# First norm of each layer and the input projection: two stages before, one stage after

## The chip, the cores and the metric

The kernel runs on one core of a Trainium2 chip. A core has five engines that run side by side and wait for one another by semaphores: TensorE (matmuls; PE in the profile, its weight loads PEld), VectorE (DVE), ScalarE (ACT), GpSimd (POOL) and SyncE (SP), which here only issues transfers (its queue is SPq). 16 DMA engines move the data. Matmuls accumulate in eight banks of PSUM, and VectorE or ScalarE copy each result out ("evacuation"). The metric is the time on the device in microseconds, the median of several runs. The profile is of one execution.

## The reference, cut to what matters

Two layers work on 1280 tokens of 1024 features: 256 context tokens and 1024 image tokens. Each layer begins with a norm and a projection:

```python
h = modulate(rmsnorm(x, norm_mix_g[l]), sh1, sc1)          # image tokens
hc = modulate(rmsnorm(xc, norm_mix_g[l]), csh1, csc1)      # context tokens, other shift and scale
parts = split_cols((h @ w_in).astype(F32))                 # 2608 columns
parts_c = split_cols((hc @ (w_in if ctx_out else w_in[:, :REC_W])).astype(F32))
...
qk = jax.nn.silu(conv2d_grid(jnp.concatenate([parts[5], parts[6]], axis=-1), conv_w, rows, cols))
```

`rmsnorm` divides by the root of the mean of the squares over a token's 1024 features; `modulate` multiplies by 1 + scale and adds shift. `ctx_out` is true in layer 0 only: in layer 1 the context tokens need no columns for the chunked gating and the Fourier mixing. Everything is float32. Mixers, output projection, a dense feed-forward part (layer 0), a mixture of eight experts (layer 1) and a final norm follow.

## The kernel before

`build` (L1976) calls one function per stage. A stage is a `Phase` (L113): a block in which each engine has its own program, and at its end a barrier of all engines; GpSimd then clears the stage's semaphores one by one. No transfer of a stage is issued before the stage ahead of it has ended. Data lies feature-major: 128 partitions, `KD` = 8 chunks of features, tokens along the row. The tokens come in three groups, `GROUPS` (L32): 256 context tokens, 512 image tokens, 512 image tokens.

`phase_norm` (L256) is the first of the two stages. SyncE loads the three groups of x (1, 2 and 2 MB) into `xT`, which lies in the space of `TM` (L271). For each group ScalarE squares eight chunks into a ring of four (L282), TensorE multiplies each square with a matrix of ones, which sums it over the partitions (L303), VectorE makes the mean plus epsilon (L312), ScalarE the root (L289), VectorE the reciprocal (L314) and the scaled chunks in place (L317), and ScalarE adds the shift and writes `hT` (L293). ScalarE's order is written out: the squares of a group stand ahead of the root and the shifts of the group before it.

`phase_project` (L322) is the second. A unit, called a tile here, is one PSUM bank: eight matmuls that sum over the chunks. Units "fm" (L400) give 128 output columns for one group of tokens, feature-major, into `FM`; units "tm" (L403) give 128 tokens by 512 columns, token-major, into `TM`. The weights come in seven blocks (four fm: q and k of the first mixer, the conv's input, the Fourier mixer's input, the gates; three tm) into a ring of two slots; a block's load waits until the last unit of the block two before it is done (L367). The gates' slot is zeroed by GpSimd first (L386), and its columns come in five small transfers (L373). The conv's taps come in four (L380). All 57 units (53 in layer 1) go block by block, context and image in each block. They use eight PSUM banks in turn; ScalarE evacuates the even units and VectorE the odd ones (L412). Between its evacuations VectorE does the 3x3 conv in twelve parts (`taps_of`, L429: four chunks, three rows of taps), and ScalarE the Silu behind it (L421).

Of the kernel before, what the change touches and what calls it, by code (L numbers as in the profile page):

```python
# [18 lines left out]
ACT = mybir.ActivationFunctionType  # L19
ALU = mybir.AluOpType  # L20
# [298 lines left out]
                            in1=rstd[:, g % 2, :n], op0=ALU.mult, op1=ALU.mult).then_inc(scaled, 1)  # L319


def phase_project(nc, io, S, l, hT, FM, TM, ctx_out):  # L322


    loads = [((0, 256), [0, 1]), ((800, 512), [2, 3, 4, 5]), ((2352, 256), [6, 7]), (None, [8])]
    tok = [(256, 0), (1312, 512), (1840, 1024)]
    w_in = io["w_in"][l].rearrange("(k p) n -> p k n", p=P)
    units = []
    for i, (_, chunks) in enumerate(loads):
        for j, ch in enumerate(chunks):  # L330
            for t0, n in GROUPS:
                if ch in (6, 7) and not ctx_out and t0 < CTX:
                    continue
                units.append((i, "fm", j, ch, t0, n))
    for i, (_, dst) in enumerate(tok):
        for n in range(NT):
            if dst == 1024 and not ctx_out and n < NCT:
                continue
            units.append((len(loads) + i, "tm", 0, dst, n, 0))
    last_of = {}  # L340
    for u, un in enumerate(units):
        last_of[un[0]] = u
    NB = 8
    with Phase(nc, f"proj{l}") as ph:
        wring = ph.sb("w", [P, 2, KD, 512])
        wl = [ph.sem(f"w_loaded{s}") for s in range(2)]
        taps = ph.sb("taps", [P, 4, 9])
        y = ph.sb("y", [P, 2, T])
        mm_done, ev = ph.sem("mm_done"), [ph.sem("evacuated_act"), ph.sem("evacuated_dve")]
        zeroed, tl, ch, cv, silu_done = (ph.sem(n) for n in ("gate_slot_zeroed", "taps_loaded", "dve_step", "convolved", "silu_done"))  # L350
        ps = S["ps"]
        nl = len(loads) + len(tok)
        cnt = {}
        need = []
        for i in range(nl):
            s = i % 2
            cnt[s] = cnt.setdefault(s, 0) + (5 if i == 3 else 1)
            need.append(16 * cnt[s])

        with nc.Block() as block:  # L360

            @block.sync
            def _(sp):
                for i in range(nl):
# [3 lines left out]
                    if i == 3:  # L368

                        sp.wait_ge(zeroed, 1)  # L370
                        with nc.allow_non_contiguous_dma(reason="gate columns"):
                            for dst, src, n in ((0, 1824, 4), (4, 1832, 4), (32, 1828, 4), (36, 1836, 4), (64, 768, 32)):
                                sp.dma_start(wring[:, s, :, dst:dst + n], w_in[:, :, src:src + n]).then_inc(wl[s], 16)  # L373
                    else:
                        c0, n = loads[i][0] if i < len(loads) else (tok[i - len(loads)][0], 512)
                        sp.dma_start(wring[:, s, :, 0:n], w_in[:, :, c0:c0 + n]).then_inc(wl[s], 16)
                    if i == 1:
                        with nc.allow_non_contiguous_dma(reason="taps as columns"):
                            for j in range(4):
                                sp.dma_start(taps[:, j, :], io["mlstm_conv"][l].rearrange("a b d -> (a b) d")[:, j * P:(j + 1) * P]  # L380
                                             .rearrange("t p -> p t")).then_inc(tl, 16)

            @block.gpsimd
            def _(pool):
                pool.wait_ge(mm_done, last_of[1] + 1)
                nc.gpsimd.memset(wring[:, 1, :, 0:P], 0.0).then_inc(zeroed, 1)  # L386

            @block.tensor
            def _(pe):
                seen = -1  # L390
                for u, (i, kind, j, dst, a, n) in enumerate(units):
                    if i != seen:
# [14 lines left out]
            def evacuate(eng, copy, u):  # L407
                i, kind, j, dst, a, n = units[u]
                eng.wait_ge(mm_done, u + 1)
                out = FM[:, dst, a:a + n] if kind == "fm" else TM[:, a, dst:dst + 512]  # L410
                src = ps[:, u % NB, :n] if kind == "fm" else ps[:, u % NB, :]
                copy(out, src).then_inc(ev[u % 2], 1)  # L412

            @block.scalar
            def _(act):
                for u in range(0, len(units), 2):
                    evacuate(act, nc.scalar.copy, u)
                    j = u // 6 - 3
                    if u % 6 == 0 and 0 <= j < 4:
                        act.wait_ge(cv, j + 1)  # L420
                        nc.scalar.activation(FM[:, 2 + j, :], y[:, j % 2, :], ACT.Silu).then_inc(silu_done, 1)  # L421
                act.wait_ge(ev[0], (len(units) + 1) // 2)
                act.wait_ge(silu_done, 4)

            @block.vector
            def _(dve):
                step = Chain(dve, ch)

                def taps_of(j, dr):  # L429
                    x, o = FM[:, 2 + j, :], y[:, j % 2, :]  # L430
                    x2, o2 = (a[:, CTX:].rearrange("p (r c) -> p r c", c=GRID_W) for a in (x, o))
                    if dr == 0:
                        dve.wait_ge(ev[0], (9 + 3 * j + 1) // 2)
                        dve.wait_ge(ev[1], (9 + 3 * j) // 2)
# [20 lines left out]
                for u in range(1, len(units), 2):  # L455
                    evacuate(dve, nc.vector.tensor_copy, u)
                    part = (u - 11) // 2
                    if 0 <= part < 12:
                        taps_of(part // 3, (0, -1, 1)[part % 3])
                for j in range(2):  # L460
                    dve.wait_ge(silu_done, j + 1)

                    step(nc.vector.tensor_scalar(FM[:, 2 + j, :], FM[:, 2 + j, :], HD ** -0.5, None, ALU.mult))
                dve.wait_ge(ev[1], len(units) // 2)


# [1620 lines left out]
```

## Time and profile before

| | us |
|---|---|
| median of 3 runs | 6105.13 (6094.68 to 6106.96) |
| profiled execution | 6100.45 |
| its span in the trace | 6098.5 |
| TensorE busy in the span | 5281.8 (87%) |
| VectorE busy | 2772.0 (45%) |
| ScalarE busy | 2003.3 (33%) |
| mean granted TensorE clock | 0.924 of full speed |

The time of the profiled execution is 2 us over its span. "Busy" counts the time in which an engine executes an instruction; matmuls are pipelined, so a busy TensorE is not one at its peak. A granted clock of 1.00 is 2.4 GHz and one of 0.50 is 1.2 GHz; a value between them means that a stretch had both. The two stages of layer 0 lie from 137 to 559 us of the span, those of layer 1 from 2206 to 2607.

### The profile page before, as it was taken

The numbers are of one execution on the slowest core, as the hardware profiler recorded it, in microseconds if no ns is written. First come the engines' busy times: TensorE is split into PE (matmuls) and PEld (weight loads), VectorE is DVE, ScalarE is ACT, GpSimd is POOL, SyncE is SP. The second block draws the span as 40 slices with busy tenths as digits, with TensorE's granted clock in tenths as the row PEclk, the third lists the DMA queues.
The fourth block names the chain that finished last, engine by engine and source line by source line (L and its number), as shares of the span: only waits on it lengthen the run. The fifth ranks groups of instructions, "written<-read, shape, count | busy, mean of one in ns | idle before, by whom it ended". The sixth has DMA issues, their size and how long they took to land. (4 is left out here: it accounts for less than half of the span.)

```text
span 6098.5 us, 61033 instructions
## 1 busy us (share of the span) xinstructions
PE 5281.8 (87%) x22972; PEld 3997.5 (66%) x22973; DVE 2772.0 (45%) x2881; ACT 2003.3 (33%) x1980; POOL 163.6 (3%) x239
## 2 busy tenths in 40 slices
PE   6899395699997969967576999999999999999994
PEld 2444174588886744425465888877887888887883
DVE  0220474311113332126524644699558644448566
ACT  1100111211112220011112534577447534437453
POOL 0000020000000000001101000000000000000001
PEclk8899697799998989978786999999999999999996
DMA  9111003211215431010227755699669755558575
GB/s 377 29 43 54 15 1 136 84 56 60 63 35 183 136 131 36 14 64 1 90 104 297 297 186 199 242 365 367 228 224 355 275 186 200 199 186 333 200 264 220
DMA packets 262623, 996.66 MB, mean 163 GB/s; under 512 B 40000, under 2 KB 112384, under 8 KB 175744
## 3 DMA queue, kind: packets, MB, share of 16 engines
q1 hardware_dynamic: 243200, 926.43, 41.4%
q0 software_dynamic: 13040, 49.29, 2.2%
q10 hardware_dynamic: 6288, 19.66, 0.8%
q8 instruction: 61, 1.00, 0.1%
q14 instruction: 34, 0.28, 0.0%
HBM read 911.68 MB, written 83.63 MB: 163 GB/s over the span
## 5 line engine op out<-in xcount | busy, mean ns | idle before, releaser
L1696 PE MATMUL ps<-moe_gate_up_hi,moe_xh 128*128 128x512 f32 x2464 | 964.9, 392 | 29.1 <-DVE moe_gate_up_lo L1841 29.1
L1696 PE MATMUL ps<-moe_gate_up_hi,moe_xl 128*128 128x512 f32 x2464 | 962.9, 391 | 0.0
L1696 PE MATMUL ps<-moe_gate_up_lo,moe_xh 128*128 128x512 f32 x2464 | 962.6, 391 | 0.0
L1841 DVE TENSOR_TENSOR moe_gate_up_lo<-moe_wst,moe_gate_up_hi 128x2048 fp32r<-128x2048 f32 x424 | 952.8, 2286 | 20.1 <-ACT moe_gate_up_hi L1774 20.1
L1774 ACT CAST moe_gate_up_hi<-moe_wst 128x2048 fp32r<-128x2048 f32 x424 | 792.1, 1922 | 0.0
L1854 DVE TENSOR_TENSOR moe_down_lo<-moe_wst,moe_down_hi 128x2048 fp32r<-128x2048 f32 x210 | 480.6, 2292 | 165.3 <-ACT moe_down_hi L1788 165.3
L1696 PEld LDWEIGHTS ps<-moe_gate_up_hi,moe_xh 128*128 128x128 f32 x2464 | 465.4, 189 | 128.3 <-DVE moe_gate_up_lo L1841 31.4
L1696 PEld LDWEIGHTS ps<-moe_gate_up_hi,moe_xl 128*128 128x128 f32 x2464 | 464.9, 189 | 97.3
L1696 PEld LDWEIGHTS ps<-moe_gate_up_lo,moe_xh 128*128 128x128 f32 x2464 | 465.3, 189 | 96.5
L1860 DVE TENSOR_TENSOR moe_a<-moe_sil,ps 128x512 f32<-128x512 f32 x210 | 143.9, 685 | 753.6 <-ACT moe_sil L1794 753.6
L1794 ACT ACTIVATE moe_sil<-ps 128x512 f32<-128x512 f32 x210 | 126.0, 600 | 1032.2 <-PE ps L1696 1032.0
L1716 PE MATMUL ps<-moe_down_hi,moe_ah 128*128 128x512 f32 x1232 | 403.1, 408 | 30.6 <-DVE moe_al L1865 30.6
L1256 PE MATMUL ps<-hh,up_wh 128*128 128x512 f32 (+1 forms) x1056 | 376.8, 357 | 51.2 <-DVE up_wl L1300 39.4
L1788 ACT CAST moe_down_hi<-moe_wst 128x2048 fp32r<-128x2048 f32 x210 | 403.7, 1922 | 22.8 <-PE ps L1716 22.7
L403 PE MATMUL ps<-proj_w,hT 128*128 128x512 f32 x928 | 398.6, 592 | 0.0
L1716 PE MATMUL ps<-moe_down_lo,moe_ah 128*128 128x512 f32 x1232 | 386.1, 395 | 0.0
L1716 PE MATMUL ps<-moe_down_hi,moe_al 128*128 128x512 f32 x1232 | 383.6, 393 | 0.0
L1256 PE MATMUL ps<-hl,up_wh 128*128 128x512 f32 (+1 forms) x1056 | 374.4, 355 | 0.0
L1256 PE MATMUL ps<-hh,up_wl 128*128 128x512 f32 (+1 forms) x1056 | 374.2, 354 | 0.0
L400 PE MATMUL ps<-hT,proj_w 128*128 128x512 f32 (+1 forms) x832 | 307.6, 533 | 48.5 <-DMA proj_w<-in_w_in 48.5
L403 PEld LDWEIGHTS ps<-proj_w,hT 128*128 128x128 f32 x928 | 176.3, 190 | 221.9 <-issue 221.9
L400 PEld LDWEIGHTS ps<-hT,proj_w 128*128 128x128 f32 x832 | 161.3, 194 | 194.9 <-issue 136.8
(329 smaller groups left out, 6497.9 us busy)
## 6 DMA issues: line engine op xcount, KB each, us to landing
moe_wst<-in_moe_packed SPq DMA_DIRECT2D x634, 1024.0 KB, 6.7
ada_w<-in_ada_packed SPq DMA_DIRECT2D x24, 2048.0 KB, 26.5
down_wst<-in_ffn_w_down SPq DMA_DIRECT2D x66, 512.0 KB, 3.6
proj_w<-in_w_in SPq DMA_DIRECT2D x8, 2048.0 KB, 7.9
four_dft<-in_dft_seq SPq DMA_DIRECT2D x16, 1024.0 KB, 4.9
xs_d<-route_zero SPq DMA_DIRECT2D x1, 16384.0 KB, 51.8
moe_rows<-xs_d POOLq DMA_DIRECT2D x16, 1024.0 KB, 5.6
ys_d<-moe_y POOLq DMA_DIRECT2D x15, 1024.0 KB, 8.5
```

The lines of the kernel that those rows point to most:

```text
L400: mm = nc.tensor.matmul(ps[:, u % NB, :n], wring[:, i % 2, k, j * P:(j + 1) * P], hT[:, k, a:a + n], start=(k == 0), stop=(k == KD - 1))
L403: mm = nc.tensor.matmul(ps[:, u % NB, :], hT[:, k, a * P:(a + 1) * P], wring[:, i % 2, k, :], start=(k == 0), stop=(k == KD - 1))
L1256: x = nc.tensor.matmul(ps[:, 2 * g + kind, :n], w[:, s, kind, k, :], h[:, k, t0:t0 + n], start=(k == 0 and j == 0), stop=(k == KD - 1 and ...
L1696: x = nc.tensor.matmul(ps[:, 2 * (q % 2) + i, :], xx[:, k, t], w[:, q % 2, k, :], start=(k == 0 and j == 0), stop=(k == KD - 1 and j == 2))
L1716: x = nc.tensor.matmul(ps[:, Y0 + 2 * i + half, :], aa[:, q % 2, i, c, :], w[:, q % 2, c, half * 512:(half + 1) * 512], start=(q == 0 and ...
L1774: nc.scalar.copy(guh[:, q % 2, 4 * j:4 * j + 4, :], wst[:, slot(n), :].rearrange("p (k n) -> p k n", k=4)).then_inc(hi, 1)
L1788: nc.scalar.copy(dnh[:, q % 2, :, :], wst[:, slot(n), :].rearrange("p (k n) -> p k n", k=2)).then_inc(hi, 1)
L1794: nc.scalar.activation(sil[:, :, :], ps[:, 2 * (q % 2):2 * (q % 2) + 2, 0:W], ACT.Silu).then_inc(silu, 1)
L1841: nc.vector.tensor_tensor(gul[:, q % 2, k, :], wst[:, slot(n), :].rearrange("p (k n) -> p k n", k=4), guh[:, q % 2, k, :].bitcast(F32), AL ...
L1854: nc.vector.tensor_tensor(dnl[:, q % 2, :, :], wst[:, slot(n), :].rearrange("p (k n) -> p k n", k=2), dnh[:, q % 2, :, :].bitcast(F32), AL ...
L1860: nc.vector.tensor_tensor(a[:, q % 2, :, :, :].rearrange("p i c f -> p i (c f)"), sil[:, :, :], ps[:, 2 * (q % 2):2 * (q % 2) + 2, W:2 * W ...
```

## The change

The two stages become one, `phase_norm_project`. x is loaded straight into `hT` and scaled and shifted there in place. The squares' ring lies in the space of `y` (the conv's buffer). One PSUM bank, number 7, is kept for the variances, and the units go round in the other seven. SyncE issues the first blocks of weights between the groups of x. The units are put in a new order: first all context units, block by block (15 in layer 0; 11 in layer 1, which has no context units in two of the blocks), then the image units of the conv's and the gates' blocks, which are in the slots at that point, then the other five blocks loaded again with their image units. The matmuls of the third group's variance stand ahead of the third unit. ScalarE alternates between a square of the next group and a shift of the present one. The number of matmuls, squares, shifts and evacuations stays.

```diff
-def phase_project(nc, io, S, l, hT, FM, TM, ctx_out):
-    loads = [((0, 256), [0, 1]), ((800, 512), [2, 3, 4, 5]), ((2352, 256), [6, 7]), (None, [8])]
-    tok = [(256, 0), (1312, 512), (1840, 1024)]
...
-    NB = 8
+def phase_norm_project(nc, io, S, l, src, hT, FM, TM, ctx_out):
+    NB, VAR = 7, 7
...
+    fm = {"qk": (0, 256, [0, 1]), "conv": (800, 512, [2, 3, 4, 5]), "four": (2352, 256, [6, 7]), "gates": (None, P, [8])}
+    tm = {"t0": (256, 512, 0), "t1": (1312, 512, 512), "t2": (1840, 512, 1024)}
+    only_out = ("four", "t2")
+    first = [n for n in ("qk", "t0", "t1", "t2", "four", "conv", "gates") if ctx_out or n not in only_out]
+    second = ["qk", "t0", "t1", "t2", "four"]
+    loads = first + second
+    GATES = len(first) - 1
+    uses = [(i, n, GROUPS[:1]) for i, n in enumerate(first)]
+    uses += [(GATES - 1, "conv", GROUPS[1:]), (GATES, "gates", GROUPS[1:])]
+    uses += [(len(first) + i, n, GROUPS[1:]) for i, n in enumerate(second)]
...
+                load_x(0)
+                for i, name in enumerate(loads):
                     s = i % 2
                     if i >= 2:
                         sp.wait_ge(mm_done, last_of[i - 2] + 1)
...
+                    if i == 0:
+                        load_x(1)
                     if i == 1:
+                        load_x(2)
...
             @block.tensor
             def _(pe):
+                def variance(g):
+                    n = GROUPS[g][1]
+                    if g:
+                        pe.wait_ge(var_ready, g)
+                    for k in range(KD):
+                        q = g * KD + k
+                        pe.wait_ge(sq_ready, q + 1)
+                        nc.tensor.matmul(ps[:, VAR, :n], ones, sq[:, q % 4, :n], start=(k == 0), stop=(k == KD - 1)).then_inc(sq_used, 1)
+
+                variance(0)
+                variance(1)
                 seen = -1
                 for u, (i, kind, j, dst, a, n) in enumerate(units):
+                    if u == 0:
+                        pe.wait_ge(shifted, KD)
+                    if u == 2:
+                        variance(2)
+                    if u == image:
+                        pe.wait_ge(shifted, 3 * KD)
...
             @block.scalar
             def _(act):
...
+                for k in range(KD):
+                    square(0, k)
+                for g in range(2):
+                    deviation(g)
+                    for k in range(KD):
+                        square(g + 1, k)
+                        shift(g, k)
+                evacuate(act, nc.scalar.copy, 0)
+                evacuate(act, nc.scalar.copy, 2)
+                deviation(2)
+                for k in range(KD):
+                    shift(2, k)
+                for u in range(4, len(units) + 8, 2):
...
             @block.vector
...
+                scale(0)
+                scale(1)
+                evacuate(dve, nc.vector.tensor_copy, 1)
+                scale(2)
...
-                    xT = TM[:, 0:7, :].rearrange("p a b -> p (a b)")[:, 0:KD * T].rearrange("p (k t) -> p k t", t=T)
-                    phase_norm(nc, S, f"nm{l}", io["xT"] if l == 0 else S["xT_d"], xT, hT, l, 0, GROUPS)
-                    phase_project(nc, io, S, l, hT, FM, TM, ctx_out)
+                    phase_norm_project(nc, io, S, l, io["xT"] if l == 0 else S["xT_d"], hT, FM, TM, ctx_out)
```

The order of instructions shows it on three engines, each at the start of the norm in layer 0. TensorE before (L303 are the variance's matmuls, L400 the first units; `cst` is the matrix of ones, `nm_sq` the squares):

```order
L303 MATMUL ps<-nm_sq,cst 128x256 [waits nm0_sq_ready] x8
L303 MATMUL ps<-nm_sq,cst 128x512 [waits nm0_sq_ready] x16
L266 UNCONDITIONAL_BRANCH
L388 UNCONDITIONAL_BRANCH [waits barrier_Pool_Activation_PE_DVE_SP_release]
L400 MATMUL ps<-hT,proj_w 128x256 [waits proj0_w_loaded0]
L400 MATMUL ps<-hT,proj_w 128x256 x7
```

And now (L423 the variance, L443 the fm units, L446 the tm units; the squares lie in `proj_y`):

```order
L423 MATMUL ps<-proj_y,cst 128x256 [waits proj0_sq_ready] x8
L423 MATMUL ps<-proj_y,cst 128x512 [waits proj0_sq_ready,proj0_var_ready]
L423 MATMUL ps<-proj_y,cst 128x512 [waits proj0_sq_ready] x7
L443 MATMUL ps<-hT,proj_w 128x256 [waits proj0_w_loaded0,proj0_shifted]
L443 MATMUL ps<-hT,proj_w 128x256 x15
L423 MATMUL ps<-proj_y,cst 128x512 [waits proj0_sq_ready,proj0_var_ready]
L423 MATMUL ps<-proj_y,cst 128x512 [waits proj0_sq_ready] x7
L446 MATMUL ps<-proj_w,hT 128x512 [waits proj0_w_loaded1]
```

The barrier between variance and units is gone, and the third group's eight variance matmuls have moved behind the first two units, ahead of the third.

ScalarE before (L282 squares, L289 root, L293 shifts):

```order
L282 ACTIVATE nm_sq<-TM 128x512 [waits nm0_sq_used] x7
L289 ACT_TABLE_LOAD
L289 ACTIVATE nm_rstd<-nm_rstd 128x256 [waits nm0_var_ready]
L293 ACTIVATE hT<-TM,mod 128x256 [waits nm0_scaled] x8
L282 ACTIVATE nm_sq<-TM 128x512 [waits nm0_sq_used,nm0_x_loaded2]
```

And now (L467 squares, L472 root, L477 shifts):

```order
L467 ACTIVATE proj_y<-hT 128x256 [waits proj0_sq_used] x4
L472 ACT_TABLE_LOAD
L472 ACTIVATE proj_rstd<-proj_rstd 128x256 [waits proj0_var_ready]
L467 ACTIVATE proj_y<-hT 128x512 [waits proj0_sq_used,proj0_x_loaded1]
L477 ACTIVATE hT<-hT,mod 128x256 [waits proj0_scaled]
L467 ACTIVATE proj_y<-hT 128x512 [waits proj0_sq_used]
L477 ACTIVATE hT<-hT,mod 128x256 [waits proj0_scaled]
```

The context root and the context shifts have moved ahead of, and in between, the second group's squares.

SyncE's queue in the joint stage of layer 0, up to the second pass (L384 x, L398 and L395 weights, L405 taps); before, the three x loads were a stage of their own:

```order
L384 DMA hT<-in_xT 128x8x256
L398 DMA proj_w<-in_w_in 128x8x256
L384 DMA hT<-in_xT 128x8x512
L398 DMA proj_w<-in_w_in 128x8x512
L384 DMA hT<-in_xT 128x8x512
L405 DMA proj_taps<-in_mlstm_conv 128x9x1 x4
L398 DMA proj_w<-in_w_in 128x8x512 [waits proj0_mm_done] x2
L398 DMA proj_w<-in_w_in 128x8x256 [waits proj0_mm_done]
L398 DMA proj_w<-in_w_in 128x8x512 [waits proj0_mm_done]
```

Two blocks of weights have moved in between the x loads.

## Rows read from the trace of the kernel before

**Rows 1.** The page's costliest groups: feature-major projection matmuls, busy, mean ns, idle before.

```profile
L400 PE MATMUL ps<-hT,proj_w 128*128 128x512 f32 (+1 forms) x832 | 307.6, 533 | 48.5 <-DMA proj_w<-in_w_in 48.5
```

**Rows 2.** Table by stretches: length, busy time and count of each engine, granted clock, DMA.

```profile
162.20:166.30 4.10, 4.01 (x5) 1.78 (x6) 0.00 (x0) 2.42 (x6) 0.00 (x0) 0.53 0.00 0
166.30:170.70 4.40, 4.40 (x12) 1.90 (x10) 1.66 (x1) 2.21 (x4) 0.00 (x0) 1.00 0.00 0
170.70:195.40 24.70, 0.56 (x3) 0.01 (x1) 16.42 (x19) 11.24 (x17) 0.00 (x0) 0.61 0.18 56
195.39:199.60 4.21, 4.21 (x10) 3.41 (x11) 0.00 (x0) 0.00 (x0) 0.00 (x0) 0.50 1.05 388
...
352.50:558.70 206.20, 206.17 (x481) 91.01 (x479) 26.83 (x31) 11.13 (x17) 0.00 (x0) 1.00 0.06 21
```

**Rows 3.** SyncE's queue in layer 0: start, duration, issues.

```profile
137.14 3.68 SPq L271 DMA_DIRECT2D TM<-in_xT  x3
190.03 1.02 SPq L376 DMA_DIRECT2D proj_w<-in_w_in  x2
...
302.21 3.59 SPq L373 DMA_DIRECT2D proj_w<-in_w_in  x5
```

**Rows 4.** TensorE in layer 0, 130 to 215 us, in order of time.

```profile
162.29 8.97 PE L303 MATMUL ps<-nm_sq,cst 128*128 128x512 f32 x16 [5.17 <-ACT nm_sq L282]
195.39 19.79 PE L400 MATMUL ps<-hT,proj_w 128*128 128x256 f32 x48 [24.14 <-DMA proj_w<-in_w_in]
```

**Rows 5.** ScalarE in layer 0's norm, in order of time.

```profile
143.73 1.33 ACT L282 ACTIVATE nm_sq<-TM 128x256 f32<-128x256 f32 x4 [12.20 <-DMA TM<-in_xT]
...
149.16 3.47 ACT L282 ACTIVATE nm_sq<-TM 128x512 f32<-128x512 f32 x6 [0.73 <-DMA TM<-in_xT]
...
154.36 1.28 ACT L289 ACT_TABLE_LOAD   x1
155.66 0.42 ACT L289 ACTIVATE nm_rstd<-nm_rstd 128x256 f32<-128x256 f32 x1
158.41 3.30 ACT L293 ACTIVATE hT<-TM,mod 128x256 f32<-128x256 f32 x8 [2.34 <-DVE TM L317]
...
173.21 5.36 ACT L293 ACTIVATE hT<-TM,mod 128x512 f32<-128x512 f32 x8 [4.21 <-DVE TM L317]
...
183.30 5.36 ACT L293 ACTIVATE hT<-TM,mod 128x512 f32<-128x512 f32 x8 [4.21 <-DVE TM L317]
```

**Rows 6.** VectorE in layer 0's norm, in order of time.

```profile
150.28 0.42 DVE L312 TENSOR_SCALAR nm_rstd<-ps 128x256 f32<-128x256 f32 x1 [14.94 <-PE ps L303]
...
157.89 3.26 DVE L317 SCALAR_TENSOR_TENSOR TM<-TM,gmod,nm_rstd 128x256 f32<-128x256 f32 x8
...
169.04 3.35 DVE L314 RECIPROCAL nm_rstd<-nm_rstd 128x512 f32<-128x512 f32 x1 [7.28 <-ACT nm_rstd L289]
```

**Rows 7.** Transfers, issue to landing: x (137), first weights (190), token-major weights (335).

```profile
TM<-in_xT SPq DMA_DIRECT2D x1, 1024.0 KB, 6.6
...
proj_w<-in_w_in SPq DMA_DIRECT2D x1, 2048.0 KB, 10.7
proj_w<-in_w_in SPq DMA_DIRECT2D x1, 1024.0 KB, 5.3
...
proj_w<-in_w_in SPq DMA_DIRECT2D x1, 2048.0 KB, 7.8
```

**Rows 8.** A conv part on VectorE (first and last row) and GpSimd's memset.

```profile
301.76 1.05 DVE L437 TENSOR_SCALAR proj_y<-FM,proj_taps 128x1280 f32<-128x1280 f32 x1
...
305.97 0.49 DVE L449 SCALAR_TENSOR_TENSOR proj_y<-FM,proj_taps,proj_y 128x255 f32<-128x255 f32 x1
...
L386 POOL MEMSET proj_w<- x2: 956/956/956, 301.2 to 2369.7; 128x1024 f32 x2
```

**Rows 9.** Layer 1: first x load, first projection matmul.

```profile
2205.86 2.98 SPq L271 DMA_DIRECT2D TM<-xT_d  x3
...
2263.96 26.63 PE L400 MATMUL ps<-hT,proj_w 128*128 128x256 f32 x72 [24.36 <-DMA proj_w<-in_w_in]
```

More of the change, by code:

```diff
@@ L319, in _ @@
                             in1=rstd[:, g % 2, :n], op0=ALU.mult, op1=ALU.mult).then_inc(scaled, 1)
-def phase_project(nc, io, S, l, hT, FM, TM, ctx_out):
-    loads = [((0, 256), [0, 1]), ((800, 512), [2, 3, 4, 5]), ((2352, 256), [6, 7]), (None, [8])]
-    tok = [(256, 0), (1312, 512), (1840, 1024)]
+def phase_norm_project(nc, io, S, l, src, hT, FM, TM, ctx_out):
+    NB, VAR = 7, 7
     w_in = io["w_in"][l].rearrange("(k p) n -> p k n", p=P)
-    units = []
[L329 to L342, printed above, removed]
-    NB = 8
+    fm = {"qk": (0, 256, [0, 1]), "conv": (800, 512, [2, 3, 4, 5]), "four": (2352, 256, [6, 7]), "gates": (None, P, [8])}
[8 more added lines that the diff above has]
+    uses += [(len(first) + i, n, GROUPS[1:]) for i, n in enumerate(second)]
+    units = []
+    for i, name, groups in uses:
+        if name in fm:
+            for j, ch in enumerate(fm[name][2]):
+                for t0, n in groups:
+                    units.append((i, "fm", j, ch, t0, n))
+        else:
+            for t0, n in groups:
+                for tile in range(t0 // P, (t0 + n) // P):
+                    units.append((i, "tm", 0, tm[name][2], tile, 0))
+    last_of = {un[0]: u for u, un in enumerate(units)}
+    image = min(u for u, un in enumerate(units) if un[1] == "fm" and un[4] >= CTX)
+    conv_in = [max(u for u, un in enumerate(units) if un[1] == "fm" and un[3] == 2 + j) for j in range(4)]
+    part_at, at = [], 0
+    for j in range(4):
+        for r in range(3):
+            at = max(at, conv_in[j])
+            at += 1 if at % 2 == 0 else 2
+            part_at.append(at)
+    silu_at = [part_at[3 * j + 2] + 3 for j in range(4)]
+    scale_at = [silu_at[j] + 2 for j in range(2)]
@@ L410, in evacuate, with square @@
                 out = FM[:, dst, a:a + n] if kind == "fm" else TM[:, a, dst:dst + 512]
-                src = ps[:, u % NB, :n] if kind == "fm" else ps[:, u % NB, :]
-                copy(out, src).then_inc(ev[u % 2], 1)
+                acc = ps[:, u % NB, :n] if kind == "fm" else ps[:, u % NB, :]
+                copy(out, acc).then_inc(ev[u % 2], 1)
             @block.scalar
             def _(act):
[L416 to L421, printed above, removed]
+                def square(g, k):
+                    t0, n = GROUPS[g]
+                    q = g * KD + k
+                    if k == 0:
+                        act.wait_ge(xl[g], 16)
+                    if q >= 4:
+                        act.wait_ge(sq_used, q - 3)
+                    nc.scalar.activation(sq[:, q % 4, :n], hT[:, k, t0:t0 + n], ACT.Square).then_inc(sq_ready, 1)
@@ new lines, in _ @@
+                for k in range(KD):
[11 more added lines that the diff above has]
+                for u in range(4, len(units) + 8, 2):
+                    if u < len(units):
+                        evacuate(act, nc.scalar.copy, u)
+                    for j in range(4):
+                        if silu_at[j] in (u, u + 1):
+                            act.wait_ge(cv, j + 1)
+                            nc.scalar.activation(FM[:, 2 + j, :], y[:, j % 2, :], ACT.Silu).then_inc(silu_done, 1)
@@ L427, in _, with scale @@
                 step = Chain(dve, ch)
+                def scale(g):
+                    t0, n = GROUPS[g]
+                    dve.wait_ge(sq_used, (g + 1) * KD)
+                    if g >= 2:
+                        dve.wait_ge(scaled, KD * (g - 1))
+                    nc.vector.tensor_scalar(rstd[:, g % 2, :n], ps[:, VAR, :n], 1.0 / D, EPS, ALU.mult, ALU.add).then_inc(var_ready, 1)
+                    dve.wait_ge(sd_ready, g + 1)
+                    nc.vector.reciprocal(rstd[:, g % 2, :n], rstd[:, g % 2, :n]).then_inc(rst, 1)
+                    dve.wait_ge(rst, g + 1)
+                    for k in range(KD):
+                        nc.vector.scalar_tensor_tensor(
+                            out=hT[:, k, t0:t0 + n], in0=hT[:, k, t0:t0 + n], scalar=gmod[:, l, 0, (1 if g == 0 else 0), k:k + 1],
+                            in1=rstd[:, g % 2, :n], op0=ALU.mult, op1=ALU.mult).then_inc(scaled, 1)
                 def taps_of(j, dr):
```

68 lines of the change are left out of this document (42 added, 26 removed).

## The prediction, written before the result was known

> **What bounds the kernel now.** The program is a row of stages with a barrier of all engines between them, so I read each stage by itself; the page's shares of busy time average over stages with different limits. Among the page's costliest groups the projection's feature-major matmuls (L400) have 48.5 us of idle TensorE before them, charged to the weight load [rows 1]. That idle time is the norm stage in front of the projection, where TensorE has only 24 small matmuls. The table by stretches shows both sides: from 170.70 to 195.40 us TensorE is busy 0.56 us of 24.7, from 352.5 to 558.7 it is busy all the time at full clock [rows 2]. So the stage pair is bound first by the norm's chain (load, squares on ScalarE, variance on TensorE, root, reciprocal and scale on VectorE, shift on ScalarE) and then by TensorE. In layer 0 the first x load is issued at 137.14 us and the first projection matmul starts at 195.39: 58.25 us [rows 3, 4]. In layer 1 it is 2205.86 to 2263.96, 58.1 us [rows 9].
>
> The unit of the sum: the token-major matmuls, two records each, fill the stretch from 352.5 to 558.7 with 480 records in 206.2 us (481 with one cut at its edge) [rows 2], so a matmul takes 0.859 us and an output tile of eight 6.87 us. A context tile of a feature-major chunk streams half as many columns and takes 3.43 us. Layer 0 has 57 such tiles, of which 15 are context: 6 token-major and 9 feature-major, 6 x 6.87 + 9 x 3.43 = 72.1 us. Layer 1 has 11: 4 x 6.87 + 7 x 3.43 = 51.5 us. The total of TensorE work is not changed.
>
> **The change, step by step, in times of layer 0 before.** *x, first group.* The context x is still the first transfer; the first square stays at 143.73, the variance is read by VectorE at 150.28 and done at 150.70 [rows 5, 6]. What could move it is the 1 MB of weights now queued behind it: nothing if transfers of one queue follow each other, 2.7 us if they share it fully (2 MB take 10.7 less 5.3 = 5.4 us, so 1 MB takes 2.7 [rows 7]). I take 0.
>
> *Root.* Before, the context root waited on ScalarE behind the eight squares of the next group, until 155.66. Now it is ahead of them. The table load (1.28 us) started the moment a square ended, ahead of the waiting instruction [rows 5], so it now runs at 148.4 to 149.7 under the last variance matmuls. The Trainium skill ("ScalarE: Activation LUTs", What ACT_TABLE_LOAD costs) gives a drain of about 1.4 us beside the load of 1.28; the trace agrees on the 1.28 and shows no such gap between load and root, and by the page the sum would still be the same here, since both end before 151.1. The root starts at 150.7; first scale 2.23 us and first shift 2.75 us behind its start, as before (155.66, 157.89, 158.41 [rows 5, 6]), that is 152.9 and 153.5.
>
> *Second group's squares, interleaved with context shifts.* Its x is 2 MB and had landed at 149.16 behind 1 MB; with 1 MB of weights ahead it lands at 151.9, about when ScalarE is free (151.1). Squares follow each other at 3.47/6 = 0.58 us, context shifts at 3.30/8 = 0.41 [rows 5], so a pair takes 0.99 and the eighth square ends at 153.5 + 0.41 + 6 x 0.99 + 0.58 = 160.4. TensorE must follow: after an idle time of some 5 us the clock was 0.53 in a stretch of 4.1 us, then 1.00 [rows 2, 4]. Cold, a variance matmul takes 1.72 us. From 154.5 on it has work without a gap: 4.1 us cold (2.4 matmuls), the other 4.6 at 0.86 give 162.6. Bounds: 161.3 if warm throughout, 166.5 if cold throughout (154.5 + 7 x 1.72). The first projection tile starts at 162.6, its weights long there, and two context tiles end at 169.5.
>
> *Third group's squares, in front of the third tile.* This is the wait that the change adds: TensorE's queue is in order and holds the other 55 tiles behind it. VectorE 0.7, ScalarE's root 0.6, then 4.2 us from the start of the 512-column reciprocal (169.04) to the first shift (173.21) [rows 5, 6]: first image shift at 168.2. The third x lands at 137.14 + 12.0 + 5 MB x 2.7 = 162.7, needed at 164. A pair is 0.58 + 5.36/8 = 1.25 us; the last square ends at 168.2 + 0.67 + 6 x 1.25 + 0.58 = 177.0, the variance at 177.9. Bounds: the same, or 183.3 if TensorE ran cold (169.5 + 8 x 1.72). I take 178.0, since it is busy 0.86 of every 1.25 us.
>
> *What this is worth.* The third tile starts at 178.0. Before, two context tiles' worth of work were done at 195.39 + 6.87 + 2.1 = 204.4, the 2.1 being half of the 4.21 us at clock 0.50 [rows 2]. So 26.4 us are gained. What remains of the norm (third group: evacuation of tile 2 at 185, root, reciprocal, scale, shift: 0.6 + 0.6 + 4.2 + 5.4 = 11 us, ready at 197) lies beside context tiles that last until 178.0 + 65.2 = 243; image tiles need it only then. In layer 1 they last until 178.0 + 44.6 = 222.6 on the same scale, still 25 us spare.
>
> *Weights.* The second pass streams 8 MB again in layer 0 and 5 MB in layer 1 (where the Fourier block and the last token-major block have no context tiles). Each load waits for the last use of its slot and has the other slot's tiles as cover: 13.7 us for the two token-major blocks of layer 0's context, against 7.8 us from issue to landing [rows 7]. One cover is thin: the conv block (2 MB) has only the Fourier block's two context tiles, 6.87 us; 7.8 + 0.3 - 6.9 = 1.2 us of wait, layer 0 only (layer 1 has a token-major block there). Without any cover it would be 8. The gate columns: memset 0.96, five issues in 3.59 us, landing at most the 5.3 of a 1 MB block [rows 3, 7, 8], 9.9 us against 13.7 of cover: 0. In the second pass the thinnest cover is the 13.7 us of the gates' image tiles. The taps stand behind all x loads and are wanted at 197: 0.
>
> *VectorE and the conv.* Its longest part, 301.76 to 306.46, is 4.7 us [rows 8] between evacuations 13.7 us apart; seven accumulators instead of eight leave six tiles of slack. The conv's last activation stands at tile 42 of 57. Cost 0; if a part were late by all seven banks it would have to last 40 us.
>
> *Boundary.* One barrier per layer goes (inside the 26.4), but its ten semaphore clears move to the end of the joint stage. ScalarE's last shift ended at 188.66 and the weights were issued at 190.03, so ten clears and a barrier are 1.37 us at most; I take 0.5 a layer, bounds 0 and 1.4. In-place shifts instead of TM to hT: the scale was in place already (TM from TM) and is no odd row among its neighbours; I take 0.
>
> Sum: layer 0 26.4 - 1.2 - 0.5 (a last bit of cold clock) - 0.5 = 24.2; layer 1 26.4 - 0.2 (58.1 against 58.25) - 0.5 - 0.5 = 25.2; together 49.4. The profiled execution took 6100.45 us, so 6051. The median of the runs is 6105.13, 4.7 above it; the new median may lie anywhere between 6051 and 6056, and I say 6053.
>
> **Rivals.** *A, the chain is slower than back-to-back rows say.* ScalarE now alternates between two producers and each instruction waits on another semaphore; x comes in between weights in one queue. If the second x lands only with the 2 MB of weights behind it (5.4 us), and TensorE stays cold through both variance passes (3.9 and up to 5.4 us), a layer loses 12 to 15 of its 25 us: about 6080; half of it 6066. For it: the clock did fall in the short pause at 157 to 162. Against: the first x landed in 6.6 us with 4 MB behind it.
>
> *B, slower: the clock stays at half in the context pass.* TensorE gets its work there in blocks between waits for squares and weights. The Trainium skill ("TensorE: Matmul & The Clock Gate", HAM oscillation) says that short bursts between waits for transfers start cold each time; our trace shows the same fall once per norm, and no case of bursts of 13 us. If all context tiles ran at 1.2 GHz, 72.1 + 51.5 = 123.6 us would double: 6051 + 124 = 6175. It turns slower than before once 50 of these 124 us are cold. Against it: from the third tile on the waits are nil but for 1.2 us, and in the rows a 4 us stretch of work brought the clock back to 1.00.
>
> *C, no difference.* The norm would have to be on the path again, for instance if the image shifts reached 243; that needs 46 us more on a chain of 11. Or weight loads in the context pass take twice as long (15.5 us against covers of 13.7 and 6.9): 2 + 2 + 9 us in layer 0, 4 in layer 1, and the gain is still about 34: no zero either.
>
> **How the numbers follow.** Forecast (gain 40 to 57) 0.78; A 0.15; B 0.03; C 0.04. A gain of under 12 us, 0.2%, is about what a measurement of this kernel can't tell from no change. Faster 0.93 (forecast and A), within 0.2% 0.04, slower 0.03. The range: upward to A's middle and a bit, 6074; downward all lower bounds (warm 1.3, free x 0.8, no conv wait 1.2, no clears 0.5) give about 6044, and the runs scatter by 12 us between them, so 6039.
>
> **What would show it.** First projection matmul some 25 us behind the first x issue instead of 58; the third tile's at 41 us, with idle TensorE before it put down to ScalarE's squares; idle before the conv context tiles of 1 us put down to the weight load in layer 0, none in layer 1; no idle TensorE after that; granted clock 1.00 from the third tile on. Wrong would be: a wait for image shifts at the first image tile, clock near 0.5 in the context tiles, or idle time in front of the gates' tile.

## The result and the profile after

| | before | after |
|---|---|---|
| median, us (4 runs each) | 6101.79 | 6048.30 (6039.77 to 6049.45) |
| ratio to before, 95% interval | | 0.991 [0.9893, 0.9927] |
| profiled execution: span, us | 6098.5 | 6037.6 |
| mean granted TensorE clock | 0.924 | 0.927 |

The kernel became 53.5 us faster by the medians. The forecast was 6053, range 6039 to 6074. The two profiled executions are 60.9 us apart. The lengths of the two stages, read in the traces from the first x issue to the next stage's first transfer, give 26.6 + 27.9 = 54.5 us of that. The other 6.4 us lie in the rest of the program, which is not changed; in the eleven profiled executions of this document that rest took 5265 to 5284 us. So the length of the stages is the measure below. The kernel after profiled twice (e5) gives it to 0.4 us in each layer, while the span differed by 18 us; e8, with the same instructions in layer 1, was 2.1 us longer there, so differences under 2 us are not read as effects.

SyncE's queue after, layer 0, then layer 1 (start, duration, issues; to be read beside [rows 3, 9]):

```profile
134.40 0.64 SPq L384 DMA_DIRECT2D hT<-in_xT  x1
...
165.73 49.47 SPq L398 DMA_DIRECT2D proj_w<-in_w_in  x4
...
531.30 0.34 SPq L580 DMA_DIRECT2D four_dftc<-in_dft_ctx  x1
...
2175.59 0.55 SPq L384 DMA_DIRECT2D hT<-xT_d  x1
...
2550.42 16.04 SPq L584 DMA_DIRECT2D four_dft<-in_dft_seq  x4
```

Layer 0 takes 531.30 - 134.40 = 396.9 us. Before it was 560.67 - 137.14 = 423.5. Layer 1: 2550.42 - 2175.59 = 374.8 against 2608.55 - 2205.86 = 402.7. The first Fourier transfers before, layer 0, then layer 1:

```profile
560.67 0.34 SPq L484 DMA_DIRECT2D four_dftc<-in_dft_ctx  x1
...
2608.55 1.29 SPq L488 DMA_DIRECT2D four_dft<-in_dft_seq  x3
```

TensorE after, layer 0, in order of time; it answers to [rows 4]:

```profile
141.49 6.10 PE L423 MATMUL ps<-proj_y,cst 128*128 128x256 f32 x16 [9.83 <-ACT proj_y L467]
150.21 8.57 PE L423 MATMUL ps<-proj_y,cst 128*128 128x512 f32 x16 [2.63 <-ACT proj_y L467]
158.62 7.07 PE L443 MATMUL ps<-hT,proj_w 128*128 128x256 f32 x32
165.53 8.07 PE L423 MATMUL ps<-proj_y,cst 128*128 128x512 f32 x16
173.44 41.36 PE L446 MATMUL ps<-proj_w,hT 128*128 128x512 f32 x96
214.64 7.07 PE L443 MATMUL ps<-hT,proj_w 128*128 128x256 f32 x32
222.65 39.85 PE L443 MATMUL ps<-hT,proj_w 128*128 128x256 f32 x132 [0.95 <-DMA proj_w<-in_w_in]
```

The first tile (158.62) starts 24.2 us behind the first x issue (58.25 before), the third (173.44) 39.0. In layer 1 they start at 2199.60 and 2214.42, 24.0 and 38.8 us behind the issue at 2175.59. Behind the third tile of layer 0 there is one wait, 0.95 us ahead of the conv block's context tiles, put down to the weight load; the gates' tile and the first image tile have none; layer 1 has none at all. The idle time ahead of the feature-major matmuls falls from 48.5 us [rows 1] to 0.9, and TensorE's work is the same: 928 and 832 records.

```profile
L446 PE MATMUL ps<-proj_w,hT 128*128 128x512 f32 x928 | 398.9, 592 | 0.0
...
L443 PE MATMUL ps<-hT,proj_w 128*128 128x512 f32 (+1 forms) x832 | 303.7, 527 | 0.9 <-DMA proj_w<-in_w_in 0.9
```

The granted clock, by stretches of layer 0 (length, busy time of each engine, clock, DMA):

```profile
150.21:153.00 2.79, 2.79 (x4) 1.04 (x5) 2.75 (x8) 2.17 (x5) 0.00 (x0) 0.50 1.04 385
153.00:158.60 5.60, 5.60 (x14) 2.51 (x13) 0.57 (x2) 4.77 (x11) 0.00 (x0) 0.99 1.05 381
158.60:165.50 6.90, 6.90 (x33) 6.07 (x32) 5.94 (x5) 2.37 (x4) 0.00 (x0) 1.00 0.37 8
165.50:173.40 7.90, 7.88 (x17) 2.69 (x17) 3.82 (x7) 7.79 (x15) 0.00 (x0) 1.00 0.76 266
```

At the start of the second group's variance it is at its lower level (0.50, 1.2 GHz) for 2.8 us, and it is at the upper one from the first tile on, which also was not so before [rows 2].

ScalarE after, around both interleavings; answers to [rows 5]:

```profile
148.08 0.42 ACT L472 ACTIVATE proj_rstd<-proj_rstd 128x256 f32<-128x256 f32 x1 [1.06 <-DVE proj_rstd L511]
149.44 0.63 ACT L467 ACTIVATE proj_y<-hT 128x512 f32<-128x512 f32 x1 [0.94 <-DMA hT<-in_xT]
150.83 0.51 ACT L477 ACTIVATE hT<-hT,mod 128x256 f32<-128x256 f32 x1 [0.77 <-DVE hT L516]
151.25 0.61 ACT L467 ACTIVATE proj_y<-hT 128x512 f32<-128x512 f32 x1
...
152.17 0.61 ACT L467 ACTIVATE proj_y<-hT 128x512 f32<-128x512 f32 x1
...
165.02 0.61 ACT L467 ACTIVATE proj_y<-hT 128x512 f32<-128x512 f32 x1
165.54 0.71 ACT L477 ACTIVATE hT<-hT,mod 128x512 f32<-128x512 f32 x1
166.15 0.61 ACT L467 ACTIVATE proj_y<-hT 128x512 f32<-128x512 f32 x1
...
185.82 5.36 ACT L477 ACTIVATE hT<-hT,mod 128x512 f32<-128x512 f32 x8 [4.21 <-DVE hT L516]
```

From square to square it is 0.92 us with context shifts (151.25 to 152.17) and 1.13 with image shifts (165.02 to 166.15). The last image shift ends at 191.2; the image tiles begin at about 240, so 49 us are spare. In layer 1 the last shift ends at 2232.2 and five context tiles from 2241.88 on still stand ahead of the image tiles, so about 27 us are spare.

### The profile page after: what moved, and what is told of

Its sections match the earlier page's. It is cut to its first block and busy times, and to the rows that moved or that the text cites. A ratio compares the mean times of both kernels' runs of the same rounds, so it can differ in the third digit from the quotient of the medians.

```text
span 6037.6 us, 61007 instructions
## 1 busy us (share of the span) xinstructions
PE 5277.5 (87%) x22972; PEld 3992.1 (66%) x22973; DVE 2770.9 (46%) x2881; ACT 2000.4 (33%) x1980; POOL 163.5 (3%) x239
## 5 line engine op out<-in xcount | busy, mean ns | idle before, releaser
L446 PE MATMUL ps<-proj_w,hT 128*128 128x512 f32 x928 | 398.9, 592 | 0.0
L1352 PE MATMUL ps<-hl,up_wh 128*128 128x512 f32 (+1 forms) x1056 | 374.5, 355 | 0.0
L446 PEld LDWEIGHTS ps<-proj_w,hT 128*128 128x128 f32 x928 | 176.3, 190 | 221.9 <-issue 221.9
L443 PE MATMUL ps<-hT,proj_w 128*128 128x512 f32 (+1 forms) x832 | 303.7, 527 | 0.9 <-DMA proj_w<-in_w_in 0.9
L1812 PEld LDWEIGHTS ps<-moe_down_hi,moe_al 128*128 128x128 f32 x1232 | 233.2, 189 | 52.8
```

The costliest lines, as they stand in the source:

```text
L443: mm = nc.tensor.matmul(ps[:, u % NB, :n], wring[:, i % 2, k, j * P:(j + 1) * P], hT[:, k, a:a + n], start=(k == 0), stop=(k == KD - 1))
L446: mm = nc.tensor.matmul(ps[:, u % NB, :], hT[:, k, a * P:(a + 1) * P], wring[:, i % 2, k, :], start=(k == 0), stop=(k == KD - 1))
L1352: x = nc.tensor.matmul(ps[:, 2 * g + kind, :n], w[:, s, kind, k, :], h[:, k, t0:t0 + n], start=(k == 0 and j == 0), stop=(k == KD - 1 and ...
L1812: x = nc.tensor.matmul(ps[:, Y0 + 2 * i + half, :], aa[:, q % 2, i, c, :], w[:, q % 2, c, half * 512:(half + 1) * 512], start=(q == 0 and ...
```

## Experiments

Theory: most of the gain is the image norm lying beside context tiles. Rivals: it is the merged stage with its early weights, or the new order on ScalarE. All lengths are from the first x issue to the next stage's first transfer, from one profiled execution each. The ratios are to runs of the kernel before made beside them.

| run | layer 0 | layer 1 | both, less the kernel after | median (ratio to before, 95%) |
|---|---|---|---|---|
| before | 423.5 | 402.7 | +54.5 | 6101.79 |
| after | 396.9 | 374.8 | 0 | 6048.30 (0.991 [0.9893, 0.9927]) |
| e1 ScalarE's order alone | 423.3 | 402.9 | +54.5 | 6107.95 (one run) |
| e2 norm first | 418.5 | 395.2 | +42.0 | 6093.95 (0.9986 [0.9976, 0.9996]) |
| e3 norm first, weights once | 417.3 | 396.8 | +42.4 | 6091.95 (0.998 [0.9971, 0.999]) |
| e4 no cover | 441.7 | 404.0 | +74.0 | 6121.81 (1.003 [1.002, 1.004]) |
| e5 after again | 397.2 | 374.5 | 0.0 | 6049.63 (0.9912 [0.9898, 0.9926]) |
| e6 VectorE adds squares | 387.1 | 364.9 | -19.7 | 6031.16 (0.9888 [0.9872, 0.9903]) |
| e7 the same, two edits more | 386.2 | 363.9 | -21.7 | 6026.76 (0.9882 [0.9867, 0.9898]) |
| e8 Fourier block second | 395.9 | 376.9 | +1.0 | 6048.44 (one run) |
| e9 x ahead of weights | 396.4 | 374.4 | -0.9 | 6045.12 (one run) |

**e1, ScalarE's order alone** (in the stage before, first norms only):

```diff
                 for g, (t0, n) in enumerate(groups):
-                    if g + 1 < len(groups):
+                    if which and g + 1 < len(groups):
                         squares(g + 1, *groups[g + 1])
...
                     for k in range(KD):
+                        if not which and g + 1 < len(groups):
+                            square(g + 1, k)
```

> The kernel before, with two stages and units block by block; only ScalarE's order in the first norm of each layer is that of the kernel after: the context root directly behind the eight context squares, then a square of the next group and a shift of the present one in turn. Theory (the gain of about 54 us is the image norm lying beside context units): the chain stays as long, the last shift of layer 0 ends some 49 us behind the first x issue instead of 51.5, and the joint length from the first x issue to the next stage's first issue falls from 423.5 to about 421; 5 us for both layers. Rival (the new order of roots, squares and shifts carries much of the gain): 10 us or more in each layer.

No gain at all: 826.2 us for both layers against 826.2 before. The norm ended only 0.8 us earlier. TensorE in layer 0 of this run:

```profile
160.33 1.12 PE L314 MATMUL ps<-nm_sq,cst 128*128 128x512 f32 x2 [1.96 <-ACT nm_sq L291]
165.26 8.74 PE L314 MATMUL ps<-nm_sq,cst 128*128 128x512 f32 x14 [3.81 <-ACT nm_sq L291]
```

Without two tiles between the second and third variance TensorE pauses 3.8 us there, and 14 records take 8.74 us instead of the 6 of full clock. The joint stage shows the same order with and without these tiles. Without them (e2 below) the third variance pauses 3.4 us and then takes 8.52 us for 14 records; with them (the kernel after) it takes 8.07 us for all 16 without a pause. It ends at the same point, 39.7 and 39.2 us behind the first x issue, so the two tiles cost the chain nothing. The rival falls, and my 5 us too.

**e2, the whole norm first**, in the joint stage:

```diff
                 variance(1)
+                variance(2)
...
                     if u == 0:
-                        pe.wait_ge(shifted, KD)
-                    if u == 2:
-                        variance(2)
+                        pe.wait_ge(shifted, 3 * KD)
```

(ScalarE and VectorE finish the third group ahead of the evacuations of the first three tiles as well.)

> The kernel after, but the whole norm stands ahead of the first unit: the third group's variance directly behind the second's, and the first unit waits for all 24 shifts. One joint stage, weights loaded beside the norm, context units first, weights streamed twice stay. Theory (overlap): the first unit starts about 49.6 us behind the first x issue (58.25 before, 24.2 after), both layers together about 15 us faster than before, 39 slower than after: about 6087. Rival (the merged stage and the early weights carry the gain): 40 us or more faster than before, about 6060.

```profile
166.79 8.52 PE L423 MATMUL ps<-proj_y,cst 128*128 128x512 f32 x14 [3.37 <-ACT proj_y L464]
186.32 9.88 PE L440 MATMUL ps<-hT,proj_w 128*128 128x256 f32 x32 [11.01 <-ACT hT L474]
```

The first tile waits for the shifts, 50.7 us behind the first x issue at 135.58 (49.6 expected). Of the 54.5 us, 12.5 remain (15 expected; by the ratio 8.5, interval 2.4 to 15), and 42.0 need the overlap. Some 4.3 of the 42 us are the clock and not the chain: behind the pause of 11 us the first two tiles take 9.88 us (8.55 in layer 1) instead of 7.07, at a granted clock of 0.50 in their first 3.7 us. The 12.5 us that remain are the merged stage and the early weights together; no run separates these two.

**e3, weights once**, otherwise as e2:

```diff
-    loads = first + second
...
+    loads = ["qk", "conv", "four", "gates", "t0", "t1", "t2"]
+    GATES = 3
+    uses = [(i, n, GROUPS if ctx_out or n not in only_out else GROUPS[1:]) for i, n in enumerate(loads)]
```

> As the run with the whole norm first, and the units again block by block with each block of weights loaded once (the conv block second, as before). Tells the price of streaming the weights twice. Theory (covered): the same as with the whole norm first within 1 us by the length of the stages (only the 0.95 us wait for the conv block in layer 0 goes): about 6086. Rival (13 MB more of transfers slow matmuls or evacuations a little everywhere): 5 us or more faster than the run with the whole norm first.

814.1 us against 813.8: streaming 13 MB more costs nothing that can be seen beyond the wait at the conv block (1.16 us in e2's layer 0). By the medians e3 is 2.0 us faster, far from the rival's 5. Layer 1 was even 1.6 us longer with less traffic: 0.7 us of that lie ahead of the first tile, 0.9 behind it, where the clock came back later (from 3.3 to 6.3 us behind the tile's start it is 0.78 in e3, and 1.00 in e2).

**e4, no cover in the context pass:**

```diff
                     if i >= 2:
                         sp.wait_ge(mm_done, last_of[i - 2] + 1)
+                    if 2 <= i <= GATES:
+                        sp.wait_ge(mm_done, max(u for u in range(ctx_units) if units[u][0] == i - 1) + 1)
```

> The kernel after, but in the context pass each load also waits for the block directly ahead of it, so no load has units to lie beside: five loads in layer 0 (t1, t2, Fourier, conv, gates), three in layer 1 (t1, conv, gates). The second pass is unchanged. Theory (each wait costs issue to landing, 7.8 us for 2 MB, 5.3 for 1 MB, about 6.5 for the gates, and after it TensorE runs at half clock for some 3 to 4 us, 1.5 to 2 us each): layer 0 plus 35.5 plus 9, layer 1 plus 22.7 plus 5, about 72 us slower than after, 6120. Rival 1 (such waits don't lower the clock): 58 slower, 6106. Rival 2 of the prediction (bursts between waits stay at half clock throughout): 58 plus most of the 96 us of context tiles behind the waits, over 6190.

TensorE, layer 0, then the clock behind the first wait:

```profile
173.85 13.90 PE L449 MATMUL ps<-proj_w,hT 128*128 128x512 f32 x32
195.75 15.82 PE L449 MATMUL ps<-proj_w,hT 128*128 128x512 f32 x32 [8.00 <-DMA proj_w<-in_w_in]
219.53 15.87 PE L449 MATMUL ps<-proj_w,hT 128*128 128x512 f32 x32 [7.96 <-DMA proj_w<-in_w_in]
240.86 8.62 PE L446 MATMUL ps<-hT,proj_w 128*128 128x256 f32 x32 [5.46 <-DMA proj_w<-in_w_in]
257.41 15.78 PE L446 MATMUL ps<-hT,proj_w 128*128 128x256 f32 x64 [7.93 <-DMA proj_w<-in_w_in]
279.04 102.67 PE L446 MATMUL ps<-hT,proj_w 128*128 128x256 f32 x240 [5.85 <-DMA proj_w<-in_w_in]
```

```profile
195.75:199.75 4.00, 4.00 (x5) 1.76 (x6) 0.00 (x0) 0.00 (x0) 0.00 (x0) 0.54 0.02 4
199.75:203.75 4.00, 4.00 (x11) 1.78 (x10) 0.00 (x0) 0.00 (x0) 0.00 (x0) 1.00 0.00 0
```

74.0 us slower than after (72 expected), and slower than before. The five waits are 35.2 us, and each puts TensorE at the lower clock: two token-major tiles take 15.8 us instead of the 13.9 ahead of the first wait. Behind the first wait the clock is back after 4 us; behind the last one of layer 0 it is 0.50 for 3.0 us and 0.65 for the next 4. In layer 1 the three waits are 21.8 us. Without the waits (and the 0.95 us that the kernel after has itself) 18 of the 74.0 us are left for eight pauses, 2.2 each; two tiles behind a pause took 1.5 to 3.0 us longer. So rival B's mechanism is real in kind, with that price per pause, not half a clock throughout; the covers keep it out of the kernel after.

**e5 to e7.** e5 is the kernel after once more. e6 takes the 24 us in front of the first tile and the 8 us in front of the third apart:

```diff
                 def variance(g):
...
-                    for k in range(KD):
-                        q = g * KD + k
-                        pe.wait_ge(sq_ready, q + 1)
-                        nc.tensor.matmul(ps[:, VAR, :n], ones, sq[:, q % 4, :n], start=(k == 0), stop=(k == KD - 1)).then_inc(sq_used, 1)
+                    pe.wait_ge(sq_used, (g + 1) * (KD - 1))
+                    nc.tensor.matmul(ps[:, VAR, :n], ones, acc[:, :n], start=True, stop=True).then_inc(var_mm, 1)
                 variance(0)
-                variance(1)
...
                     if u == 2:
+                        variance(1)
+                    if u == 5:
                         variance(2)
...
+                def presum(g):
+                    for k in range(1, KD):
...
+                        nc.vector.tensor_tensor(acc[:, :n], acc[:, :n], sq[:, r % 4, :n], ALU.add).then_inc(sq_used, 1)
```

(`presum` is VectorE's; the first square of a group lies in `acc`.) Two more things differ in e6 and e7, so they do not price the adds alone. The second group's variance stands behind the first two tiles and the third group's behind the fifth. And ScalarE no longer takes squares and shifts in turn: it does the context shifts ahead of the second group's squares, and the image shifts between the first and the last four of the third group's; tile 0 is evacuated earlier too. e7 adds this:

```diff
-    first = [n for n in ("qk", "t0", "t1", "t2", "four", "conv", "gates") if ctx_out or n not in only_out]
+    first = [n for n in ("qk", "four", "t0", "t1", "t2", "conv", "gates") if ctx_out or n not in only_out]
...
+                    if g == 0:
+                        sp.dma_start(hT[:, 0:4, t0:t0 + n], src[:, 0:4, t0:t0 + n]).then_inc(xl[g], 16)
+                        sp.dma_start(hT[:, 4:8, t0:t0 + n], src[:, 4:8, t0:t0 + n]).then_inc(xh, 16)
```

> The kernel after once more, beside the two versions below on the same chip: its ratio to before again near 0.991, the stage lengths again 396.9 and 374.8 us (422.6 less 0.7 and so on: 26.6 and 27.9 shorter than before).

> The kernel after, but VectorE adds up the eight squares of a group, and TensorE multiplies only the sum by the ones: 3 variance matmuls a layer instead of 24. The first unit follows the context shifts directly, the second group's variance stands ahead of the third unit, the third group's ahead of the sixth. Theory (the 24 us in front of the first unit and the 8 us in front of the third are the chain of squares through TensorE, which runs it at half clock at first): first unit at about 18.7 us behind the first x issue instead of 24.2, third unit at 28.5 instead of 39.0, about 9.7 us a layer net of the moved variance, 19 us faster than after, about 6029. Rival (VectorE becomes the bound: seven adds of 0.7 us per group delay scale and evacuations, and TensorE waits for a bank or for image shifts; or the clock falls in the longer pause ahead of the first unit and stays down): same as after or slower.

> As the run with VectorE adding the squares, and two more edits: the context x comes in two halves with a semaphore each, and the Fourier block stands second in the context pass (its 1 MB in front of the third x, and every 2 MB block covered by a 2 MB block). Theory: first square 1.5 us earlier in each layer, the 0.95 us wait for the conv block in layer 0 gone; 3 to 4 us faster than without them, about 6025. Rival: the first squares are not on the path (the adds or the x of the second group are) and only 1 us comes.

TensorE in e6, layer 0 (first x issue at 135.97):

```profile
146.24 1.22 PE L423 MATMUL ps<-proj_y,cst 128*128 128x256 f32 x2 [13.01 <-DVE proj_y L518]
154.07 9.61 PE L444 MATMUL ps<-hT,proj_w 128*128 128x256 f32 x32 [6.61 <-ACT hT L480]
163.51 1.02 PE L423 MATMUL ps<-proj_y,cst 128*128 128x512 f32 x2
164.37 20.76 PE L447 MATMUL ps<-proj_w,hT 128*128 128x512 f32 x48
```

First tile at 18.1 us, third at 28.4 (18.7 and 28.5 expected); 19.7 us off both stages (19 expected), 18.5 by the medians of runs made together. TensorE has 14 matmuls of 512 columns less ahead of and between its tiles, 12.0 us a layer at 0.859 each; 9.9 us a layer came out. No run separates the adds from the new places and the new order on ScalarE. VectorE's seven adds take 5.47 us for a 512-column group and TensorE waits for none of the image groups' in e6. The context group's (3.61 us) are on the path: they end 1.7 us behind the last square, and the first variance matmul waits for them. The rival's clock came in part: behind a pause of 6.61 us the first two tiles take 9.61 us (9.20 in layer 1) instead of 7.07.

e6 is faster than both kernels. e7 is 2.0 us shorter than e6 by the lengths, which is no more than their scatter, and 4.4 us faster by the medians (3 to 4 expected), though one of its four runs, 6032.47, was slower than all of e6's; that it gains over e6 is likely, not shown. In e7 the context x came in two halves (first square 4.1 us behind the issue, 5.9 in e6, 6.6 after), but layer 0 has a new wait of 0.82 us for VectorE's adds at the third variance, and the Fourier block in second place opened another:

```profile
160.73 7.07 PE L449 MATMUL ps<-hT,proj_w 128*128 128x256 f32 x32
169.00 7.13 PE L452 MATMUL ps<-proj_w,hT 128*128 128x512 f32 x16 [1.20 <-DMA proj_w<-in_w_in]
```

Its 2 MB block behind was issued at 160.07 and took 8.9 us to land, with 7.8 us of work as cover: the 8 us of variance matmuls that covered it in e8 are gone here.

**e8, the Fourier block second**, in the kernel after:

```diff
-    first = [n for n in ("qk", "t0", "t1", "t2", "four", "conv", "gates") if ctx_out or n not in only_out]
+    first = [n for n in ("qk", "four", "t0", "t1", "t2", "conv", "gates") if ctx_out or n not in only_out]
```

> The kernel after with one edit: the Fourier block second in layer 0's context pass instead of fifth. Theory (the 0.95 us wait for the conv block is its thin cover of two context tiles): the wait is gone, no new one appears since the 2 MB block behind it has 6.9 us of tiles and 8 us of variance as cover; stage of layer 0 about 1 us shorter than 396.9, layer 1 unchanged at 374.8. Rival (the wait is the conv block's own slow landing): it stays.

```profile
174.98 7.07 PE L443 MATMUL ps<-hT,proj_w 128*128 128x256 f32 x32
181.89 41.36 PE L446 MATMUL ps<-proj_w,hT 128*128 128x512 f32 x96
223.09 113.56 PE L443 MATMUL ps<-hT,proj_w 128*128 128x256 f32 x304
```

No wait is left in layer 0's rows, and the stage is 1.0 us shorter, as expected. Layer 1 has the same instructions as after and was 2.1 us longer: 14 records of its second variance took 8.90 us instead of 7.07, with the granted clock at 0.50 for 4 us and 0.66 for 2 more. So the stage lengths carry a scatter of up to 2 us, and e8's 1.0 us rests on the missing wait, not on the length alone.

**e9, x ahead of the weights:**

```diff
                 load_x(0)
+                load_x(1)
+                load_x(2)
                 for i, name in enumerate(loads):
```

> The kernel after with one edit: all three x loads are issued ahead of the first block of weights. In the kernel after ScalarE waited 0.94 us for the second x and 0.23 for the third in layer 0. Theory (these waits are not on the path, since the second square is followed by the context shifts that wait for VectorE, and TensorE catches up; what sets the first unit is the clock at which it does the variance matmuls): the second group's first square 0.9 us earlier, the first unit at 23.5 to 24.5 us behind the first x issue (24.2 in the kernel after), stage lengths within 1 us of 396.9 and 374.8. Rival (weights in front of x cost their transfer time, 2.7 us for the second x and 8 for the third): first unit at about 21.5 and stages 3 us shorter.

First tile at 23.8 and 23.6 us, stages 0.5 and 0.4 us shorter: within the scatter. The second group's first square came 1.2 us earlier, the first tile only 0.4 us: the 0.94 us of waiting for the second x was not on the path, and the 3 us of the rival are not there.

## Why the prediction held, and where its sum was off

- *Which stretch is worth the time.* Right: e2 keeps the merged stage, the early weights and the new orders, and gets 12.5 of 54.5 us. The 42 us come with the tiles that run while the norm of the image tokens goes on.
- *The front of the chain.* First square 6.6 us behind the issue, context variance read at 13.2, first scale at 15.9: all within 0.2 us of the forecast. The table load ran right behind the eighth square, under the last variance matmuls, as said. The second x landed at 15.0 (14.8 expected). The third landed at 26.0 (25.6 expected), and ScalarE waited 0.23 us for it where none was expected.
- *First tile 25.5 forecast, 24.2 and 24.0 measured; third tile 40.9 forecast, 39.0 and 38.8 measured.* Two terms were mis-sized. The cold spell at the second variance lasted 2.8 us, not 4.1, and TensorE caught up with the squares, as in the forecast's lower bound (161.3, which is 24.2 behind the issue). And ScalarE's pairs take 0.92 and 1.13 us, where I had summed 0.99 and 1.25 from rows of one operation repeated. My 0.58 for a square included waits inside the row of six: a row of four squares without waits takes 2.17 us, 0.52 from start to start. An image shift stands 0.61 ahead of the next square, not 0.67. The last square of the third group ended at 38.0 us, 39.9 forecast, and with it came nearly all of the third tile's 1.9.
- *From the third tile on.* The 0.5 us of cold clock that I set aside in each layer did not come. 1.9 (third tile) + 0.25 (conv wait) + 0.5 - 0.2 (clears) = 2.4 in layer 0 makes the forecast 24.2 into 26.6. In layer 1, 25.2 became 27.9: 2.3 us come from the same terms (2.0 + 0.5 - 0.2), and 0.4 are not accounted for. So the sum of 49.4 us was 5.1 short of 54.5. The forecast of 6053 lies 4.7 us above the measured median. That the two differences agree so well is chance, since the four runs after scatter over 10 us.
- *Conv wait* 1.2 us forecast, 0.95 measured (0.86 to 1.16 in the runs that keep the order), 0 in layer 1; *gates* 0, measured 0; *second streaming* 0, and e3 shows none within the scatter.
- *Boundary.* TensorE's pause into the Fourier stage went from 2.05 to 2.77 us, 0.7 for ten more clears; I had 0.5 within 0 and 1.4. e6 has one semaphore more to clear and e7 two: 2.84 and 2.91 us, 0.07 for each, which fits.
- *Rivals.* A: neither of its pieces appeared (the second x was on time, the third variance ran at full clock); the chain was faster than the rows had said. B: e4 shows the clock falling at each pause and coming back within 3 to 6 us, so it needs pauses that the covers prevent. C: the image shifts had 49 us to spare, 27 in layer 1.

## What to carry to other kernels

A stage that prepares its operands in groups can start its matmuls on the smallest group, if the others' preparation is shorter than that group's matmuls; price it as the start of the first matmul that has no gap behind it, not as the length of the preparation. Streaming 13 MB of weights a second time cost nothing above the scatter of 2 us, since each block's matmuls covered the next block's load; each uncovered load cost its landing time (5.5 to 8.0 us in e4) plus 1.5 to 3.0 us of lower clock. In front of a TensorE-bound stage look at the small matmuls too: summing the squares on an idle VectorE, with the variances moved behind tiles, took another 19.7 us.

## What the runs showed of the hardware that was not expected

- TensorE's clock fell in a pause of 2.6 us: it was 0.74 in the 2.6 us of variance matmuls ahead of it and 0.50 for 2.8 us behind it. Behind pauses of 3.8 to 11 us it was lower for about 3 to 6 us. The same instruction stream gave stage lengths 2.1 us apart, all of it ahead of the first tile, where the clock came back later (layer 1 of the kernel after and of e8).
- ScalarE overlaps a square with a shift as well as two of a kind: squares started 0.52 us ahead of the following shift though each took 0.61.
- The taps' four small transfers took 15.1 us to issue behind 8 MB of loads (12.7 to 16.9 in the other runs), 10.2 behind 3 MB before. Nothing waited for them, but the next block's load stands behind them in the queue: in e6 and e7 the last one was out only 0.4 and 0.7 us before the tiles freed the slot for that load.
- Each semaphore more that was cleared between two stages lengthened TensorE's pause there by 0.07 us (2.77, 2.84, 2.91).
